# Raw rows transposed ahead of the last output quarter, with the root-mean-square factor applied behind the matmuls

## The reference, cut to what matters

```python
def rms_norm(x, g):
    return x * rsqrt(mean(x * x, -1) + 1e-6) * g

for i in range(4):                     # layers a0, b, c, a1
    hn = rms_norm(x, norm[i])
    x = x + mixer(hn, ...)

def conformer_conv_mixer(h, ...):      # a0, a1
    val, gate, z = split(h @ w_in, 3)  # 2048 columns each
    u = causal_conv31(val * sigmoid(gate)) + conv_b
    return (silu(layer_norm(u)) * silu(z)) @ w_out

def forgetting_attention_mixer(h, ...):   # b, 16 heads of 128
    q, k, v, z, f = split(h @ w_in)       # f: 16 columns
    q, k = rms_norm(q per head), rms_norm(k per head)
    c = cumsum(log_sigmoid(f + f_bias))
    p = softmax(causal(q @ k.T / sqrt(128) + c[t] - c[s]))
    return ((p @ v) * silu(z)) @ w_out

def short_conv_mixer(h, ...):          # c
    u, b, cg, z = split(h @ w_in, 4)
    return (b * causal_conv3(cg * u) * silu(z)) @ w_out
```

## Time and profile before

| | us |
|---|---|
| device time, median of 3 runs | 1759.94 (1759.84 to 1760.04) |
| the profiled execution, its own time | 1759.21 |
| its span | 1757.4 |

### The profile page before, as it was taken

One profiled execution on the slowest core, in us unless ns is written; L12 is line 12 of the kernel. 1 busy time (PEld: TensorE's weight loads), 2 busy tenths in 40 slices (PEclk: granted clock), 3 DMA queues, 4 the chain that ended last, 5 costly groups with the idle time before them and its releaser, 6 DMA issues.

```text
span 1757.4 us, 28644 instructions
## 1 busy us (share of the span) xinstructions
PE 1720.6 (98%) x10400; PEld 1505.8 (86%) x10400; DVE 1473.6 (84%) x2856; ACT 1091.4 (62%) x2145; POOL 288.3 (16%) x396
## 2 busy tenths in 40 slices
PE   8999999999999999999999999999999999999997
PEld 7888888888888888888898988988888998988886
DVE  7999878877789999778987698789987688789887
ACT  6888665555465555578875455566666656566664
POOL 2996000000000000078920000002000200002000
PEclk9999999999999999999999999999999999999999
DMA  6455568855558898544465654546764544546662
GB/s 236 145 159 186 168 220 302 272 172 180 200 196 311 288 308 301 192 145 136 153 192 156 226 182 133 169 146 190 259 212 151 168 157 126 175 141 188 223 187 78
DMA packets 92733, 339.48 MB, mean 193 GB/s; under 512 B 10288, under 2 KB 10672, under 8 KB 91952
## 3 DMA queue, kind: packets, MB, share of 16 engines
q1 hardware_dynamic: 92592, 337.64, 58.9%
HBM read 336.55 MB, written 1.05 MB: 192 GB/s over the span
## 4 chain that ended last, share of the span: by engine, by line
PE 74%; DVE 12%; ACT 9%; issue 3%; POOL 2%; DMA 0%; SPq 0%; ACTq 0%; DVEq 0%; POOLq 0%
PE ps L104 72%; ACT tmp L110 4%; DVE wl L120 4%; ACT wh L113 2%; PE ps L107 2%; POOL B L120 2%; DVE tmp L130 1%; DVE raw L130 1%; DVE tmp L120 1%; DVE B L120 1%; ACT os L113 1%; DVE sm L142 1%; ACT B L110 1%; DVE tmp L125 1%; DVE os L120 1%
## 5 line engine op out<-in xcount | busy, mean ns | idle before, releaser
L104 PE MATMUL ps<-XS,wh 128*128 128x256 f32 (+2 forms) x3120 | 767.1, 327 | 8.5 <-DVE wl L120 4.5
L120 DVE TENSOR_TENSOR wl<-raw,wh 128x1024 fp32r<-128x1024 f32 x467 | 572.4, 1240 | 101.5 <-ACT wh L113 99.3
L104 PE MATMUL ps<-XS,wl 128*128 128x256 f32 x2120 | 572.6, 281 | 0.0
L104 PEld LDWEIGHTS ps<-XS,wh 128*128 128x128 f32 (+1 forms) x3120 | 515.2, 190 | 64.4 <-issue 18.6
L113 ACT CAST wh<-raw 128x1024 fp32r<-128x1024 f32 x467 | 475.6, 1045 | 101.4 <-PE ps L104 92.5
L104 PEld LDWEIGHTS ps<-XS,wl 128*128 128x128 f32 x2120 | 402.1, 190 | 11.5
L120 POOL TENSOR_TENSOR B<-B,tmp 128x236 f32<-128x236 f32 (+11 forms) x368 | 246.0, 711 | 643.2 <-ACT tmp L110 627.3
L104 PE MATMUL ps<-wh,os 128*128 128x512 f32 x864 | 279.6, 392 | 5.0 <-DVE B L133 2.1
L104 PE MATMUL ps<-B,raw 128*128 128x256 f32 x1056 | 232.7, 380 | 0.0
L104 PEld LDWEIGHTS ps<-B,raw 128*128 128x128 f32 x1056 | 198.8, 190 | 29.5 <-issue 3.4
L130 DVE SCALAR_TENSOR_TENSOR ps<-B,C,ps 128x253 f32<-128x253 f32 (+17 forms) x560 | 216.6, 474 | 2.8 <-ACT ps L110 2.8
(11 more groups left out here) (165 smaller groups left out, 1665.1 us busy)
## 6 DMA issues: line engine op xcount, KB each, us to landing
raw<-in_w SPq DMA_DIRECT2D x628, 512.0 KB, 4.4
B<-in_ln SPq DMA_DIRECT2D x4, 1024.0 KB, 6.1
C<-in_cst SPq DMA_DIRECT2D x1, 1103.5 KB, 9.1
X<-in_x SPq DMA_DIRECT2D x2, 512.0 KB, 4.5
out_x<-X SPq DMA_DIRECT2D x4, 256.0 KB, 2.5
cb<-in_cb SPq DMA_DIRECT2D x1, 512.0 KB, 12.8
pos<-in_pos SPq DMA_DIRECT2D x1, 160.0 KB, 5.3
raw<-in_w SPq DMA_DIRECT2D x1, 128.0 KB, 2.1
```

What stands on the lines that cost most here:

```text
L104: return NOTHING if self.e is None else self.e.matmul(*a, **k)
L120: return NOTHING if self.e is None else self.e.tensor_tensor(o, a, b, op)
```

## The change

In a0, b, c and a1, the un-normalized rows of X are transposed. The output quarters of the layer before now come in the order (0,0), (1,0), (0,1), (1,1), and eight of the sixteen transposes stand ahead of the last quarter, since they need only the first half of the channels. The other eight are spread behind the first steps of the next layer. R is formed meanwhile, spread over partitions on PE (`pe_row_root`), copied by ACT into 256 columns of G (Rb in the code), and applied behind the matmuls:

- a0, a1: the first gate pair g0 multiplies un-normalized tiles (`taken`) and its result is multiplied by Rb. Eight DVE multiplies give the normalized tiles xn for the rest. In a1, the pieces g1.0 and g1.1 become split instead of plain. a0's filler matmuls, on constants that are loaded, become 18 on a small block that DVE fills; the bias tables' first steps (`dve_bias_begin`) move ahead of xn.
- b: f's logit is multiplied by Rb in one more DVE operation; the v copies take R as their scale; q's and k's own norms get a scaled epsilon instead. The z of each head is multiplied by Rb in a DVE operation (`gated`) that ACT's tanh waits for, and which itself waits for the head's values matmuls. f's matmuls are interleaved with v0's steps, and the small transposing matmul `b.ct` moves from behind v0 to behind v1. `values(3)` moves ahead of the quotients of step 3.
- c: the product of c and u is multiplied by the square of Rb, z by Rb, and b's factor is left to the residual, which takes R as its scalar. Both multiplies are DVE operations of 128x512, one each per pair. Of the first pair's ada pieces, two come behind all four projections.

The filler matmuls of b, c and a1 are gone.

```diff
     def out_last(self, pe, L, ks, Ys):
-        for tb in range(2):
-            for h in range(2):
-                for k, Y in zip(ks, Ys):
+        for tb, h in self.quarters(L):
+            if tb and h and L in ("a0", "b", "c"):
+                for k in range(4):
+                    self.pe_raw_turned(pe, {"a0": "b", "b": "c", "c": "a1"}[L], k)
+            for k, Y in zip(ks, Ys):
...
+    def pe_row_root(self, pe, L):
+        pe.wait_ge(*self.s["norm"][L, "root"])
+        self.spread(pe, 7, self.sums("R"), (L, "R"))
+
+    def act_row_root(self, act, L):
+        act.wait_ge(*self.s["spread"][L, "R"])
+        act.activation(self.row_root(), self.ps[7][:, 0:T], ACT.Identity).then_inc(self.s["evac"].up((L, "R")), 1)
...
 # layer a, DVE
+        Rb, g0 = self.row_root(), self.tmp[0].rearrange("p (a t) -> p a t", a=2)
+        dve.wait_ge(*s["evac"][A, "R"])
+        for k in range(8):
+            dve.wait_ge(*s["norm" if k in (1, 2) else "shift"][A, "raw", k])
+            dve.tt(self.xn()[:, k, :], self.taken(k), Rb, ALU.mult).then_inc(s["norm"].up((A, "xn", k)), 1)
+        dve.wait_ge(*s["gemm"][f"{A}.g0.1"])
+        dve.tt(g0, self.ps[4].rearrange("p (a t) -> p a t", a=2), Rb.unsqueeze(1).to_broadcast([128, 2, T]),
+               ALU.mult).then_inc(s["norm"].up((A, "g0")), 1)
...
 # layer b, PE
+        pe.wait_ge(*s["soft"]["b", "y"])
+        self.token_major(pe, self.b_chunk(1), "b.v1", "b")
+        pe.wait_ge(*s["soft"]["b", "cc"])
+        for k in range(2):
+            ins = pe.matmul(self.ps[2][:, 16 * k:16 * k + 16], cc[0:16, 128 * k:128 * k + 128], I16, start=True, stop=True)
+        ins.then_inc(s["small"].up("b.ct"), 1)
+        pe.wait_ge(*s["soft"]["b", "ct"])
+        self.token_major(pe, self.b_chunk(2), "b.v2", "b")
 # layer b, DVE
+        dve.tt(y, self.ps[6][0:32, 0:T], Rb[0:32, :], ALU.mult).then_inc(s["soft"].up(("b", "yr")), 1)
...
+        def gated(h):
+            dve.wait_ge(*s["value"]["b", h])
+            dve.tt(self.b_z(h), self.ps[6 + h % 2][:, T:2 * T], Rb, ALU.mult).then_inc(s["evacd"].up(("b", "z", h)), 1)
...
+            if 0 <= h < 16:
+                gated(h)
             if 2 <= h:
                 self.feed_dve(dve, f"b.o{h - 2}")
 # layer b, ACT
-            act.wait_ge(*s["value"]["b", h])
+            act.wait_ge(*s["evacd"]["b", "z", h])
 # layer c, DVE
+            dve.tt(cs.rearrange("p (a t) -> p a t", a=2), cs.rearrange("p (a t) -> p a t", a=2),
+                   square.unsqueeze(1).to_broadcast([128, 2, T]), ALU.mult).then_inc(s["evacd"].up(("c", "u", i)), 1)
             self.feed_dve(dve, f"c.b{i}.1")
...
+            dve.tt(zs2, zs2, Rb.unsqueeze(1).to_broadcast([128, 2, T]), ALU.mult).then_inc(
+                s["evacd"].up(("c", "z", i)), 1)
```

More of the change, by code:

```diff
@@ L212, in plan_a @@
     for p in range(8):
-        two("g", p, E, "plain", "plain")
+        two("g", p, E, *["split" if j and p == 1 else "plain"] * 2)
         two("v", p, 0, "split" if p else "plain", "plain")
@@ L264, in plan_c @@
                     out.append((f"c.{kind}0.{n}", tiles("c_w_in", 0, base + n * 128), "split"))
-                    if kind == "u":
-                        ada()
+            for n in range(2):
+                ada()
         for kind, base in (("c", 2 * E), ("u", 0), ("b", E), ("z", 3 * E)):
@@ new lines, in pe_raw_turned @@
+    def pe_raw_turned(self, pe, L, k):
+        s, h, a = self.s, k // 4, (k % 4) * 128
+        if L != "a0" and k >= 4:
+            pe.wait_ge(*s["resid"][self.prior(L), 1, 1])
+        for tb in range(2):
+            pe.wait_ge(*(s[f"x{tb}"][0] if L == "a0" else s["resid"][self.prior(L), tb, h]))
+            ins = pe.transpose(self.turned_tile(L, k)[:, tb * 128:tb * 128 + 128], self.half(tb, h)[:, a:a + 128],
+                               self.c("ident", 0, 128))
+        ins.then_inc(s["turn"].up((L, "in", k)), 1)
@@ L733, in act_squares @@
         for tb in range(2):
-            for h in range(1 if tb and L == "a0" else 2):
+            for h in range(2):
                 act.wait_ge(*ready(tb, h))
@@ L739, in act_squares @@
         self.act_root(act, self.sums("d"), self.sums("v"), L)
[L741 to L757, removed]
@@ L922, in act_a, with highs @@
         order = [self.taps(p) for p in range(8)]
+        def highs():
+            for k in range(8):
+                act.wait_ge(*s["norm"][A, "xn", k])
+                act.copy(self.xh(k), self.xn()[:, k, :]).then_inc(s["high"].up((A, k)), 1)
         if j == 0:
-            self.act_rms(act, A, lambda tb, h: s[f"x{tb}"][0], "a_norm0", True)
+            act.table(ACT.Sqrt)
+            self.act_square(act, A, 0, 0)
+            self.act_square(act, A, 0, 1)
+            self.act_square(act, A, 1, 0)
+            self.act_taken(act, A, 0)
+            self.act_taken(act, A, 3)
+            self.act_root(act, self.sums("d"), self.sums("v"), A)
+            for k in range(4, 8):
+                self.act_taken(act, A, k)
+            self.act_row_root(act, A)
+            highs()
             act.wait_ge(*s["cb"][0])
@@ L929, in act_a @@
         else:
-            self.act_rms(act, A, lambda tb, h: s["resid"]["c", tb, h], "a_norm1", True)
+            act.table(ACT.Sqrt)
+            self.act_square(act, A, 0, 0)
+            self.act_taken(act, A, 0)
+            self.act_square(act, A, 1, 0)
+            self.act_square(act, A, 0, 1)
+            self.act_taken(act, A, 3)
+            self.act_square(act, A, 1, 1)
+            self.act_root(act, self.sums("d"), self.sums("v"), A)
+            for k in range(4, 8):
+                self.act_taken(act, A, k)
+            self.act_row_root(act, A)
+            highs()
         w_conv, b_conv = f"a_conv_w{j}", f"a_conv_b{j}"
@@ L1815, in act_c @@
         s = self.s
-        self.act_rms(act, "c", lambda tb, h: s["resid"]["b", tb, h], "c_norm", False)
+        act.table(ACT.Sqrt)
+        self.act_square(act, "c", 0, 0)
+        self.act_turned_high(act, "c", 0)
+        self.act_turned_high(act, "c", 1)
+        self.act_turned_high(act, "c", 2)
+        self.act_square(act, "c", 1, 0)
+        self.act_turned_high(act, "c", 3)
+        self.act_square(act, "c", 0, 1)
+        self.act_square(act, "c", 1, 1)
+        self.act_turned_high(act, "c", 4)
+        self.act_root(act, self.sums("d"), self.sums("v"), "c")
+        for k in range(5, 8):
+            self.act_turned_high(act, "c", k)
         def split(i):
```

333 lines of the change are left out of this document (219 added, 114 removed).

## The result

The changed kernel takes 1777.75 us (median of 4 runs, 1775.82 to 1778.12) against 1759.99 us (1759.84 to 1760.46): 17.8 us slower. The ratio of the means is 1.0098, 95% interval 1.0086 to 1.0111 (ratios here are of means, differences in us of medians). The forecast was 1772.6 us, 12.7 us slower, in a range of 1760 to 1779.

The account below looks back on a forecast made before the run. It took DVE to pace b's softmax and c's pairs, DVE and POOL a0, and PE only a1. Terms summed to +12.7 on the profiled 1759.21, giving 1771.9; with 0.7 for the median, 1772.6 us, range 1760 to 1779.

Parts of the forecast that it names:

- a0, +2.0: Layer a0: gates start earlier, but DVE's longer chain makes the low parts 2.2 us later; 2.0 us slower in all.
- b's entry, +1.9: Start of layer b: fillers go, but f's late logit delays v1's casts, PE waits about 3.8 us; 1.9 us slower.
- b's softmax, +8.5: Layer b's 16 heads: z's added DVE multiply lengthens DVE's row and delays the tanh; 8.5 us slower.
- c's entry, -1.4: Start of layer c: without fillers the first units end 3.05 us early, partly given back; 1.4 us faster.
- pairs, +5.3: Layer c's pairs: added multiply costs 0.65 us in seven pairs, z's multiply 0.73 at the last output; 5.3 us slower.
- a1, -3.6: Layer a1, paced by PE: first value product 2.4 us earlier, two split gate pieces save 1.2; 3.6 us faster.
- Rival C: Forecast plus TensorE at its lower pace after the wait at v1, +2.3 us: 1774.9 us; chance 0.13.
- Rival A: Whole kernel: added vector work is covered by DVE's idle time, leaving the entries' gains, -9.4 us: 1750.5; chance 0.12.
- Rival B: Entries gain 7.75 us, half to all of softmax and pairs' 13.8 is paid: 1759.1 to 1766.0 us; chance 0.15.

Follow-up runs that it names:

- a0 alone: The kernel before with the change in layer a0 only, b, c and a1 in the old code: 1763.95 us, ratio 1.0020.
- the fillers: The changed kernel with 16 filler matmuls on PE between v1's first and second piece in layer b: 1773.72 us.
- a1 alone with fillers: The kernel before with a1's change, plus 8 fillers ahead of a wait in b's third head and 7 ahead of c's last output steps: 1755.13 us.
- a1 alone: The kernel before with the change in layer a1 only, including its two split gate pieces: 1757.95 us, ratio 0.9981.
- c alone: The kernel before with the change in layer c only: 1764.67 us, ratio 1.0024.
- the multiply on other data: The changed kernel with each softmax head's z multiply replaced by an equal-sized DVE multiply that waits for nothing and nobody awaits: 1769.93 us.
- b alone: The kernel before with the change in layer b only: 1772.86 us, ratio 1.0072.
- no multiply: The changed kernel with z's multiply by the root left out in b's softmax: 1764.79 us.
- on POOL: The changed kernel with z's softmax multiply moved from DVE to POOL, after an ACT copy of z from PSUM: 1777.15 us.
- without the multiplies in c: The changed kernel with layer c's two multiplies per pair (c*u by the squared root, z by the root) left out: 1769.78 us.

## Why the prediction was right, and where it was off

The direction and the mechanism were right: added DVE work is paid in full where DVE or its chain paces, and an entry's gain arrives only where PE does. Step by step:

- **a0, +2.0.** It is 1.15. The list of DVE's work was right and somewhat too long: the root's copy came at 12.99 instead of 13.9, and xn's multiplies at 13.47, so that the low parts ended at 19.8 instead of 20.4. The first value product on DVE started at 28.66, where 29.5 was foretold and 27.48 was before. The step missed that the delay makes longer waits in PE's row, 1.9 us near 45 and 2.0 near 165. In this execution the clock stayed up behind both; with a0 alone the second cost 1.4.

```profile
13.47 2.77 DVE L120 TENSOR_TENSOR B<-B,G 128x256 f32<-128x256 f32 x8 [2.13 <-issue]
...
17.06 2.76 DVE L120 TENSOR_TENSOR XS<-B,XS 128x256 fp32r<-128x256 f32 x8
```

- **b's entry, +1.9.** The wait was foretold at about 3.8 us and is 3.85. The +3.7 is 1.9 and 1.8 of clock, shown by the fillers. The match of the 1.9 is partly luck, for the sum has slips: its cast at 245.3, with 1.3 and a low part of some 1.2 behind it, ends at 247.8 and not 247.5, and a wait of 3.8 less a gain of 2.75 makes v1 1.05 late and not 0.75. The forecast laid the wait to the log-sigmoid's place ahead of the casts. Preparing the piece ahead of it removed the wait there and bears that out, but it came back as 2.94 us at the next piece: DVE's row behind the log-sigmoid was late as well.
- **b's softmax, +8.5.** It is 9.4, with a period of 8.61 us where 8.4 to 8.6 was foretold. The steady heads came as foretold, the edges partly by luck. The sum had 9.7 for the multiply (2.0 for the first two heads, 6.0, and 1.7 at the end) and 0.9 of it absorbed by PE's old wait in head 2. The runs show 11.1 for the multiply and 1.7 gained without it. So two errors offset.
- **c's entry, -1.4, and pairs, +5.3.** They are -1.7 and +6.0. The entry's own terms, 1.95 less 0.72, make -1.2 and not the -1.4 written there. Each of the seven pairs comes 0.75 later, not 0.65, so the margin of up to 0.15 was not there. The last wait was foretold at 2.6 and is 2.55.
- **a1, -3.6.** It is -2.2 in this execution, for the clock fell at 744.9, and -3.8 with the clock up (a1 alone with fillers).
- **Rival C** (chance 0.13) is the main part of what lifted the result from 1772.6 to 1777.75. It was priced once, at 2.3 us, for one place (20 passes at 0.10 more are 2.0). The other terms' errors leave some 0.5 us in the profiled execution. In that execution the slower clock came at two places (1.8 at v1, and about 1.6 in c's last wait), and the mean granted clock of the other three runs is 0.992 to 0.993 against 0.994. A lower mean by 0.0015 is 2 x 0.0015 x 1775 = 5.3 us more at half clock, or up to 2.7 us of time, which is about the 1.9 by which the median lies above the profiled run. Which wait that was in them, no profile shows. What failed is that the slower clock was set at nothing in the sum and kept for a rival: a term of 1.8 for v1, and 1.6 for c's last wait, which no rival had. The rule cited there from the Trainium skill, page "TensorE: Matmul & The Clock Gate", part 1, that an idle array is put back to half rate, agrees with the trace here (0.51 in the stretch from 246.5), and the result lies with it. Not every wait was followed by a fall: behind 2.94 us in the kernel with v1's piece prepared early, the clock stayed up.
- **Rival A** (0.12), by occupancy, falls: without the softmax's multiply the kernel's median is 13 us lower, although DVE is busy 84% in both. By the rule of the Trainium skill, page "Perfetto Trace Analysis", section "Identifying the Most-Contended Engine", as the prediction read it, the multiply would have been covered; the traces go against that here.
- **Rival B** (0.15), the charges in part, falls too: softmax and pairs came to 15.4 us, where 13.8 was foretold as the whole.

Not settled: why a wait of some 2 us drops the clock in one execution and not in the next (1.89 us before: no; 1.86 with a1 alone: yes; 2.62 with c alone: no; 2.55 changed: yes), nor why 2.98 near 46 in the kernel without the multiply was followed by no fall and 2.99 at the same place, in the one with the multiply on other data, by 6.8 us at half.

## What to carry to other kernels

Work that is moved off an entry onto a later operation is paid as often as that operation runs: ask for each layer which engine's row of work paces it, and put the factor only where PE paces. An engine that is busy 84% can be the pacing one, if its idle time consists of waits for its own results on another engine's way back. When a change opens a wait of some 2 us or more on PE, put the slower matmuls behind it into the sum, weighed by the chance that the clock falls and only where PE paces what follows. Try fillers in the waits that are there anyway. And where the runs of a kernel fall into groups by their mean clock, compare group with group.

## What the runs showed of the hardware that I had not expected

- Waits of PE of 1.83 to 2.06 us were followed by 3.4 us at half clock in some executions and not in others. Near 165 and 389 us and at c's end such a stretch cost about 1.4 to 1.6 us, near 46 nothing. The wait of some 3.85 us at v1 was followed by 6.8 us at half in five traces (the changed kernel, b alone, no multiply, on POOL, without the multiplies in c) and by 3.4 us in a sixth (the multiply on other data).
- The kernel before has two groups of run times, 1759.2 to 1760.1 (18 runs, mean clock 0.996 to 0.997) and 1761.7 to 1762.4 (9, mean clock 0.995 to 0.996), in the first group of experiments; with 15 fillers in two waits the upper group was absent from 11 runs.
- A DVE subtraction of 128x1024 took 1.75 us instead of 1.22 beside a POOL multiply of 128x256, which took 1.12 us; it was so nine times in the 16 heads.
